# A reordered convolution tail and feed-forward entry in a two-layer decoder step

## What is computed

```python
# layer 0: convolution mixer
a = h @ w_pw1 + b_pw1
u = a[..., :D] * sigmoid(a[..., D:])
y = causal_depthwise_conv(concat(prev, u), w_dw, width=31) + b_dw
y = silu(layernorm(y, ln_g, ln_b))
x = x + m2 * (y @ w_pw2)
# both layers: feed-forward
a = h @ w_up                              # 1024 -> 2 x 2816
x = x + m5 * ((silu(a[..., :F]) * a[..., F:]) @ w_down)
# between the layers: keys and values, blocks of 32 tokens compressed
pr = einsum('bnlkd,lde->bnke', xp, w1[seg]) + einsum('ld,lde->e', pe[seg], w1[seg])
# layer 1: sparse attention on compressed, selected and window keys
```

## Time and profile before

| | us |
|---|---|
| median of 3 runs | 1714.19 |
| lowest, highest | 1709.68, 1717.39 |
| the profiled execution | 1709.89 |
| its span, first to last instruction | 1708.2 |

### The profile page before, as it was taken

How to read it: one execution, slowest core, us unless ns; L and a number is a source line. 1 busy time by engine, 2 the same in 40 slices (tenths; PEclk the granted TensorE clock), 3 DMA queues, 4 the chain that set the end, 5 groups by cost and what they waited for, 6 DMA issues and landing times.

```text
span 1708.2 us, 34694 instructions
## 1 busy us (share of the span) xinstructions
PE 1573.8 (92%) x13817; PEld 1427.1 (84%) x13817; DVE 1144.3 (67%) x2319; ACT 781.7 (46%) x1644; POOL 164.7 (10%) x284
## 2 busy tenths in 40 slices
PE   5888898989999999999999999888898999999996
PEld 3887777989999999989999655455788999999995
DVE  5899976675766858774253467566368676775865
ACT  4545557443453525443224555454344444452544
POOL 2000001000020000002100345333100000000000
PEclk8999999999999999998999999888999999999997
DMA  9889970313645443523322500100232232333321
GB/s 323 273 296 323 303 223 21 88 50 112 198 132 137 124 124 112 146 77 101 79 70 72 153 26 2 50 26 26 75 88 61 63 105 82 100 87 92 95 75 56
DMA packets 236923, 198.40 MB, mean 116 GB/s; under 512 B 7570, under 2 KB 196322, under 8 KB 236496
## 3 DMA queue, kind: packets, MB, share of 16 engines
q1 hardware_dynamic: 225360, 162.81, 31.9%
q0 software_dynamic: 6352, 23.88, 4.7%
q10 hardware_dynamic: 5056, 9.54, 1.7%
HBM read 188.87 MB, written 11.20 MB: 117 GB/s over the span
## 4 chain that ended last, share of the span: by engine, by line
PE 75%; DMA 8%; DVE 7%; ACT 5%; issue 4%; POOL 1%; POOLq 0%; SPq 0%; DVEq 0%; ACTq 0%
PE ps L2215 31%; PE ps L2529 23%; DMA ada<-in_w_ada_dram 6%; PE ps L2195 5%; PE ps L2266 4%; PE ps L2231 3%; PE ps L2663 2%; PE ps L2710 2%; PE ps L2588 2%; DMA xrows<-in_x_sample_dram 1%; DVE t L1483 1%; PE ps L2780 1%; DMA C<-in_cache_kv_dram 1%; PE ps L2564 1%; DVE PT L2115 1%
## 5 line engine op out<-in xcount | busy, mean ns | idle before, releaser
L820 ACT ACTIVATE wh<-raw 128x1024 fp32r<-128x1024 f32 (+2 forms) x129 | 118.6, 921 | 287.7 <-PE ps L2215 263.3
L2529 PE MATMUL ps<-Hh,bh 128*128 128x288 f32 x608 | 179.6, 295 | 2.0 <-DVE t L1887 2.0
L2529 PE MATMUL ps<-Hh,bl 128*128 128x288 f32 x608 | 179.0, 294 | 0.0
L2529 PE MATMUL ps<-Hl,bh 128*128 128x288 f32 x608 | 179.0, 294 | 0.0
L2215 PE MATMUL ps<-Hh,wh 128*128 128x288 f32 (+1 forms) x688 | 156.1, 309 | 13.6 <-DVE wl L1415 9.0
L2215 PE MATMUL ps<-Hl,wh 128*128 128x288 f32 (+1 forms) x688 | 150.7, 301 | 0.0
L2215 PE MATMUL ps<-Hh,wl 128*128 128x288 f32 (+1 forms) x688 | 150.3, 301 | 0.0
L1415 DVE TENSOR_TENSOR wl<-raw,wh 128x1024 fp32r<-128x1024 f32 (+2 forms) x129 | 135.1, 1049 | 14.7 <-ACT wh L820 14.3
L2215 PE MATMUL ps<-ah,wh 128*128 128x288 f32 x656 | 140.8, 296 | 2.2 <-issue 2.1
L2215 PE MATMUL ps<-al,wh 128*128 128x288 f32 x656 | 140.2, 295 | 0.0
L2215 PE MATMUL ps<-ah,wl 128*128 128x288 f32 x656 | 140.2, 295 | 0.0
(11 more groups left out here) (381 smaller groups left out, 3889.7 us busy)
## 6 DMA issues: line engine op xcount, KB each, us to landing
ada<-in_w_ada_dram SPq DMA_DIRECT2D x55, 1024.0 KB, 8.4
raw<-in_ffn_w_up_dram SPq DMA_DIRECT2D x88, 512.0 KB, 4.9
raw<-in_conv_w_pw_dram SPq DMA_DIRECT2D x24, 512.0 KB, 9.2
raw<-in_ffn_w_down_dram SPq DMA_DIRECT2D x32, 384.0 KB, 3.8
raw<-in_ffn_w_down_dram SPq DMA_DIRECT2D x32, 320.0 KB, 3.3
ada<-in_w_ada_dram ACTq DMA_DIRECT2D x9, 1024.0 KB, 7.1
raw<-in_w_kv_dram SPq DMA_DIRECT2D x12, 512.0 KB, 3.9
C<-in_cache_kv_dram POOLq DMA_DIRECT2D x32, 128.0 KB, 3.6
```

The lines of the kernel that those rows point to most:

```text
L820: A(wh[:, u % RING, 0:K, 0:w], raw[:, u % RING, 0:K, 0:w], ACT.Copy).then_inc(hi_ready, 1)
L2529: last = M(ps[:, bank, 0:HT], wt[:, blk, k], rt, start=(j in (0, 1, 2, 6) and k == 0 and i == 0), stop=(k == 3 and i == 2), skip_group_che ...
```

## The change

- Tail of the convolution: y of chunks 0 to 6 is summed by POOL into `mu` (`add_chunk`), PE sums that total and chunk 7 only. Groups 2 and 3 of `up4` and `us4` for chunk 7 are copied by 16 POOL DMAs, groups 0 and 1 by ACT; DVE copies no `us4` for it and writes `stage` instead of ACT. The last strip is turned after the sums and evacuated after the norm. The square root table is loaded before the convolution ends.
- Norms that precede a feed-forward load the silu table once the first half is done.
- Feed-forward entry: on DVE the first split and `product(0)` come after two of the five inner sums, the second split after the third, the third split after the fifth. On ACT the third split comes one place earlier.
- The first pair of a section waits for its banks one by one, by the unit number modulo 3.
- `cmp_bias` is gone; `pe_cmp` becomes 15 more columns of the first hidden product, and ACT takes the bias from one of them.
- `expd` and `tabs` share the semaphore `sel_in`; `slopes` is merged into `const`.

The diff, cut to its core:

```diff
@@ -543,7 +544,7 @@
...
                    8: [("hidden", 1)]}
-        CMP_END = {2: [("bias", 0)], 3: [("turn", 1)], 4: [("turn", 3)], 5: [("keys", 0)], 6: [("turn", 5)],
+        CMP_END = {3: [("turn", 1)], 4: [("turn", 3)], 5: [("keys", 0)], 6: [("turn", 5)],
@@ -690,8 +691,33 @@
...
+            def add_chunk(j):
+                pool.wait_ge(S("conv"), (CW + 1) * (j + 1))
+                pool.wait_ge(S("cs_ev"), j + 1)
+                if j > 1:
+                    pool.wait_ge(S("taps_in"), 2 + j - 1)
+                nc.gpsimd.tensor_tensor(mu[:], y[:, 0, :] if j == 1 else mu[:], y[:, j, :], ALU.add).then_inc(S("taps_in"), 1)
+
+            pool.wait_ge(ada_ev, 4 * (STRIPS_FIRST + 2))
+            for j in range(1, DC - 2):
+                add_chunk(j)
+            pool.wait_ge(S("taps_in"), 2 + DC - 3)
...
             nc.gpsimd.memset(up4[96:P, :, TP + 4 * STEPS - 8:], 0.0).then_inc(S("const"), 1)
+            pool.wait_ge(S("const"), 5)
+            pool.wait_ge(tile_free, U_PW2)
+            for g in range(2, 4):
+                for sh in range(4):
+                    n = min(TP + 4 * STEPS - 4, CW - 1 + TP - sh)
+                    pool.dma_start(up4[32 * sh:32 * sh + 32, g, 0:n], u_p[32 * g:32 * g + 32, DC - 1, sh:sh + n]).then_inc(S("up4_dma"), 16)
+            pool.wait_ge(S("cs_pe"), DC - 1)
+            for g in range(2, 4):
+                for sh in range(4):
+                    n = (CW - 1 + NT - sh) * NB
+                    pool.dma_start(us4[32 * sh:32 * sh + 32, g, 0:n],
+                                   u_s[32 * g:32 * g + 32, DC - 1, sh:, :].rearrange("p t b -> p (t b)")).then_inc(S("us4_dma"), 16)
+            pool.wait_ge(S("const"), 5)
+            add_chunk(DC - 2)
@@ -772,12 +798,12 @@
...
             pool.wait_ge(tile_done, U_WO)
-            pool.dma_start(expd[:], c["expd"]).then_inc(S("expd_in"), 16)
+            pool.dma_start(expd[:], c["expd"]).then_inc(S("sel_in"), 16)
...
-            pool.dma_start(tabs[:], c["tabs"]).then_inc(S("tabs_in"), 16)
+            pool.dma_start(tabs[:], c["tabs"]).then_inc(S("sel_in"), 16)
@@ -943,6 +969,9 @@
...
                 else:
+                    if keeps:
+                        act.wait_ge(S("st_tb"), g + 2 + (g + 1) // 2)
+                        A(scrap[:], epst[:], ACT.Silu).then_inc(S("st_tb"), 1)
@@ -1087,23 +1116,24 @@
...
             act.wait_ge(tile_free, U_PW2)
-            for g in range(4):
+            for g in range(2):
...
                     A(up4[32 * sh:32 * sh + 32, g, 0:n], u_p[32 * g:32 * g + 32, DC - 1, sh:sh + n], ACT.Copy).then_inc(S("up4_in"), 1)
-                if g == 1:
-                    sample_out(DC - 2)
+            sample_out(DC - 2)
+            for g in range(2):
+                for sh in range(4):
+                    n = (CW - 1 + NT - sh) * NB
+                    A(us4[32 * sh:32 * sh + 32, g, 0:n], u_s[32 * g:32 * g + 32, DC - 1, sh:, :].rearrange("p t b -> p (t b)"),
+                      ACT.Copy).then_inc(S("us4_in"), 1)
...
             s_ += STRIPS_TAIL
-            strip_out(None, s_ - 1)
+            A(scrap[:], epst[:], ACT.Sqrt)
...
             sample_out(DC - 1)
-            act.wait_ge(S("cr_pe"), 1)
-            A(stage[0:CW - 1, 0, :].rearrange("p (b f) -> p b f", b=2), ps[0:CW - 1, 0:2, :], ACT.Copy).then_inc(S("cr_ev"), 1)
-            A(stage[0:TS, 1, :].rearrange("p (b f) -> p b f", b=2), ps[0:TS, 2:4, :], ACT.Copy).then_inc(S("cr_ev"), 1)
@@ -1123,8 +1153,7 @@
...
-            A(scrap[:], epst[:], ACT.Sqrt)
-            act.wait_ge(S("ln_pe"), DC)
+            act.wait_ge(S("ln_pe"), 2)
@@ -1134,6 +1163,7 @@
...
             ln_hi(1)
+            strip_out(None, s_ - 1)
@@ -1208,8 +1238,8 @@
...
                 inner_hi(layer, 0)
+                split_hi(u0 + 2 + SPLIT_AHEAD)
                 high(0)
-                split_hi(u0 + 2 + SPLIT_AHEAD)
@@ -1260,23 +1290,19 @@
...
                         act.wait_ge(S("kc_pe"), 1)
+                    if g2 == 0:
+                        A(peb[:, t:t + 1], ps[:, 6 + t, n:n + 1], ACT.Copy).then_inc(S("hc"), 1)
+                        act.wait_ge(S("hc"), 2 * t + 1)
...
-            def cmp_bias():
-                act.wait_ge(S("hp_pe"), 1)
-                A(peb[:], ps[:, 6, 0:2], ACT.Copy).then_inc(S("hc"), 1)
-                act.wait_ge(S("hc"), 1)
-
             def cmp_prompt(t):
-                act.wait_ge(S("hp_pe"), 2 + t)
+                act.wait_ge(S("hp_pe"), 1 + t)
...
                 for what, arg in steps:
-                    if what == "bias":
-                        cmp_bias()
-                    elif what == "turn":
+                    if what == "turn":
@@ -1727,13 +1753,10 @@
...
-            dve.wait_ge(S("cs_pe"), DC - 1)
-            dve.wait_ge(tile_free, U_PW2)
-            for g in range(4):
-                for sh in range(4):
-                    n = (CW - 1 + NT - sh) * NB
-                    V.tensor_copy(us4[32 * sh:32 * sh + 32, g, 0:n],
-                                  u_s[32 * g:32 * g + 32, DC - 1, sh:, :].rearrange("p t b -> p (t b)")).then_inc(S("us4_in"), 1)
+            dve.wait_ge(S("cs_pe"), DC)
+            dve.wait_ge(S("cr_pe"), 1)
+            V.tensor_copy(stage[0:CW - 1, 0, :].rearrange("p (b f) -> p b f", b=2), ps[0:CW - 1, 0:2, :]).then_inc(S("cr_ev"), 1)
+            V.tensor_copy(stage[0:TS, 1, :].rearrange("p (b f) -> p b f", b=2), ps[0:TS, 2:4, :]).then_inc(S("cr_ev"), 1)
@@ -1892,15 +1915,15 @@
...
                 inner_sum(layer, 1)
+                split_lo(u0 + SPLIT_AHEAD)
+                product(0)
                 inner_sum(layer, 2)
+                split_lo(u0 + 1 + SPLIT_AHEAD)
...
                 inner_sum(layer, 4)
-                product(0)
-                split_lo(u0 + SPLIT_AHEAD)
-                split_lo(u0 + 1 + SPLIT_AHEAD)
+                split_lo(u0 + 2 + SPLIT_AHEAD)
...
                 low(0)
-                split_lo(u0 + 2 + SPLIT_AHEAD)
@@ -1991,6 +2014,13 @@
...
+            def offsets():
+                for t, cp in enumerate((CPk, CPv)):
+                    pe_t = vT[:, R_PE + 16 * t:R_PE + 16 * t + 16].rearrange("p (r f) -> p f r", r=2)
+                    V.tensor_copy(cp[:, :, 4 * NKV, 0:2], pe_t)
+                    V.memset(cp[:, :, 4 * NKV, 2:], 0.0)
+
+            offsets()
@@ -2382,7 +2412,9 @@
...
                 pe.wait_ge(S("taps_in") if j < 2 else S("taps_dve"), j + 1 if j < 2 else j - 1)
-                pe.wait_ge(S("us4_in"), 16 * (j + 1))
+                pe.wait_ge(S("us4_in"), 16 * (j + 1) if j < DC - 1 else 16 * j + 8)
+                if j == DC - 1:
+                    pe.wait_ge(S("us4_dma"), 16 * 8)
@@ -2413,19 +2445,11 @@
...
-            def sum_y(cc):
-                pe.wait_ge(S("cs_ev"), cc + 1)
-                pe.wait_ge(S("conv"), (CW + 1) * (cc + 1))
-                sum_chunk(y[:, cc, :], cc, S("ln_pe"), bank=4)
-
-            for cc in range(DC - 2):
-                sum_y(cc)
-
             pe.wait_ge(S("taps_dve"), DC - 2)
-            pe.wait_ge(S("up4_in"), 16)
+            pe.wait_ge(S("up4_in"), 8)
+            pe.wait_ge(S("up4_dma"), 16 * 8)
             pe.wait_ge(S("cs_ev"), DC - 1)
-            turn_strip(s_ - 1)
-            pe.wait_ge(ada_ev, 4 * s_)
+            pe.wait_ge(ada_ev, 4 * (s_ - 1))
@@ -2433,10 +2457,12 @@
...
             convs += 1
-            sum_y(DC - 2)
+            pe.wait_ge(S("taps_in"), 2 + DC - 2)
+            sum_chunk(mu, 0, S("ln_pe"), n=2, bank=4)
...
             pe.wait_ge(S("pc_ev"), 1)
-            sum_chunk(y[:, DC - 1, :], DC - 1, S("ln_pe"), bank=4)
+            sum_chunk(y[:, DC - 1, :], 1, S("ln_pe"), n=2, bank=4)
+            turn_strip(s_ - 1)
@@ -2499,8 +2525,11 @@
...
                         if j == 0:
-                            pe.wait_ge(tile_free, q.before)
+                            pe.wait_ge(tile_free, q.before - (q.before % RING > 0))
                         elif j == 2:
+                            pe.wait_ge(tile_free, q.before + (q.before % RING == 1))
+                    elif q.i == 1:
+                        if j == 0:
@@ -2556,24 +2585,16 @@
...
-            def cmp_bias():
-                pe.wait_ge(S("w1_in"), 32)
-                pe.wait_ge(S("st_rms"), 5)
-                for t in range(2):
-                    for j in range(LC // 2):
-                        last = M(ps[:, 6, t:t + 1], w1s[t][:, j, :], vT[:, R_PE + 16 * t + j:R_PE + 16 * t + j + 1],
-                                 start=(j == 0), stop=(j == LC // 2 - 1))
-                last.then_inc(S("hp_pe"), 1)
-                pe.wait_ge(S("hc"), 1)
-
...
                 pe.wait_ge(S(f"cc_in{b % 2}"), 64 * (b // 2 + 1))
+                if b == 0:
+                    pe.wait_ge(S("st_rms"), 5)
...
                     pe.wait_ge(S("kc_dve"), 2)
-                    pe.wait_ge(S("hc"), 3)
+                    pe.wait_ge(S("hc"), 4)
@@ -2582,23 +2603,25 @@
...
                 pe.wait_ge(S("cp_act"), 4 * g2 + 4)
-                n = 4 * NKV * NCS
```

(13 more changed lines are left out.)

33 lines of the change are left out of this document (16 added, 17 removed).

## The result

The changed kernel takes 1696.42 us, median of four runs (1694.59 to 1700.01), against 1715.79 of the kernel before, ratio 0.9898, 95% interval 0.9868 to 0.9929. A second group gave 1696.49 against 1716.08, ratio 0.9882 (0.9849 to 0.9916). So the change makes the kernel faster by 1.0 to 1.2%, 19.4 to 19.6 us by the medians, where the forecast had 23.8. The forecast of 1688.0 was 8.4 too low; the measured time lies in its range of 1680 to 1698 and outside of its own forecast's 1683 to 1693.

What follows compares the result with a forecast made beforehand. It took PE's own work, three quarters of the span, and PE's standstills as the bound; terms for tail, feed-forward entries, key/value projection and attention start summed to -23.8 us, giving 1688, range 1680 to 1698 (8 in 10).

Steps and rivals of the forecast that it cites:

- start of the prompt convolution: Convolution tail: with fewer ACT copies and the sums off PE, the last prompt convolution starts at 244.7, not 248.79: -4.1.
- square root table: End of the convolution tail: table load and dummy activation move into ACT's idle time before the convolution ends: -1.5.
- entry of feed-forward 0, PE's start: Feed-forward 0 entry: with the new DVE order and early silu table, PE starts at 356.74, not 360.78: -4.0.
- clock and bank wait behind it: Feed-forward 0 after its entry: full clock with a 0.6 gap, -2.2, and the first pair's bank wait gone, -0.8.
- keys and values: Key and value projection: bias products go, hidden product grows 0.8, full clock returns; nothing is late next: -11.3.
- attention: wait, clock: Attention start: the gate product waits for tabs too, +4.5, and the idle drops the clock, +1.4.
- entry of feed-forward 1: Second feed-forward entry: PE starts 4.0 earlier and full clock gives 1.8; no bank gain.
- hidden by ACT: Convolution tail: the eight up4 transfers end at 242 to 243 (doubled bound 244.1), before ACT is done; no cost.
- The rival of late transfers: Convolution tail: up4 transfers end at 249, leaving only the table gain: -19.7, about 1692; 13%.
- The two on tabs: Attention start: wait for tabs absorbed, -29.7, about 1682, 10%; or costs +12 instead of 5.9, about 1694, 12%.
- The one on the order at the entries: Feed-forward entries: half of each 4.0 and the clock return as a wait one unit later; about 1694; 8%.
- The one that ends slower: Convolution tail: POOL's 16 SBUF copies run one after another, +60; kernel about 1751, slower than before; 3%.

Runs made afterwards that it cites:

- b_order: Kernel before with only the new order of splits, product and sums on VectorE and ScalarE at both feed-forward entries; 1710.98 us, ratio 0.9955.
- b_bias: Kernel before with only the bias folded into the first hidden product; 1700.52 us, ratio 0.9897.
- c_pages: Changed kernel with the gate product waiting for expd alone and the turns of the cache pages spread; 1680.75 us, ratio 0.9777.
- a_expd: Changed kernel with tabs on another semaphore, so the gate product waits for expd alone; 1692.39 us.
- a_oldentry: Changed kernel with the old order of splits, product and sums at both feed-forward entries, silu table still early; 1707.82 us, ratio 0.9954 to the kernel before.
- a_thin: Changed kernel with five of POOL's six adds cut to one column; 1693.66 us, ratio 0.988 to the kernel before.
- c_filler: c_pages plus ten unused products of y with ones on PE before the last prompt convolution; 1678.27 us, ratio 0.9798 to the kernel before.
- f_short: c_pages plus five unused products on PE before the last prompt convolution; 1679.59 us, ratio 0.9815 to the kernel before.

## Why the prediction was right and wrong

Each term of the sum against what the stages show. "Measured" is the mean with the edit less the mean without it, over the profiles above that differ in nothing else in that stage.

| term | forecast | measured |
|---|---|---|
| start of the prompt convolution | -4.1 | -3.8 |
| square root table | -1.5 | -0.2 |
| clock in the sums of squares | 0 | -1.7 |
| entry of feed-forward 0, PE's start | -4.0 | -3.8 |
| clock and bank wait behind it | -3.0 | -2.4 |
| given back up to keys and values | 0 | +1.4 |
| keys and values | -11.3 | -8.4 |
| attention: wait, clock | +4.5, +1.4 | +4.9, +1.7 |
| entry of feed-forward 1 | -5.8 | -5.3 |
| from there to the end | 0 | +0.4 |
| sum | -23.8 | -17.2 |

The timings say 19.4 and 19.6, with intervals that reach from 12 to 26.

**The base, 4.0 of the 8.4.** "The profiled run took 1709.9 ... the median of the three runs is 4.3 higher ... I take the middle". The middle, 1711.8 as it stands in the forecast (1688 + 23.8), was too low: the median of before was 1715.8 with one run more, and 1712 to 1722 in four groups. The profiled execution was 0.2 above the lowest of the three shown, and a profile at the lower end is no evidence on the level of the next runs. The median less 23.8 would have been 1690.4.

**The rest, 4.4, is the effect.** The step that failed is "What is late next is nothing", for keys and values, and with it the term of 11.3, which measured 8.4 (9.3 if b_order, which has no edit in this stage, is counted with the kernels before). The weights were there, but I did not ask for the pages of the cache, though PE's waits for them stand in the trace of before, at the fourth and the eighth turn:

```profile
806.53 1.09 PE L2195 MATMUL ps<-ident,C 128*128 128x128 f32 x8 [1.38 <-DMA C<-in_cache_kv_dram]
844.54 1.09 PE L2195 MATMUL ps<-ident,C 128*128 128x128 f32 x8 [1.54 <-DMA C<-in_cache_kv_dram]
```

The removal and the fold are right: the first turn comes 12.1 earlier (39.47 becomes 27.35; 9.86 + 0.26 + 2.0 were summed), the stretch that holds the hidden product takes 0.8 more (20.01 becomes 20.83), and b_bias gives 11.9 alone. In the changed kernel the two page waits are 2.0 to 3.1 each and behind one or both of them the clock falls (the eight turns took 1.97 instead of 1.09 at 825.45): the stage is 3.5 longer than in b_bias. c_pages takes the waits away and finds 6.4. That the removal makes them longer is not shown, and two profiles speak against it: b_bias has the removal and short waits, b_order has none and long ones. First b_bias, then b_order:

```profile
801.19 1.09 PE L2199 MATMUL ps<-ident,C 128*128 128x128 f32 x8 [1.54 <-DMA C<-in_cache_kv_dram]
803.36 1.36 PE L2195 MATMUL ps<-ident,C 128*128 128x128 f32 x8 [2.47 <-DMA C<-in_cache_kv_dram]
```

Against b_order the changed kernel's stage is 11.2 shorter, against before b_bias's is 11.9 shorter. So the removal is worth what was forecast either way; what is missing is a wait that the sum held constant and that came out longer. Why is open, below.

**The clock term was put in the wrong places.** I gave the clock back where a long wait goes, and this held at both entries (46.98 against 48.88 with nothing else changed) and behind tabs. I did not ask the same question where work is removed: the six sums that leave PE had kept it busy up to the last prompt convolution. With an idle of 2.5 to 3.2 before it, that convolution took 8.61 to 8.77 (four profiles), with 0.6 to 1.5 it took 7.07 in seven of eight. The eighth is a_expd, 9.35 behind an idle of 0.98:

```profile
245.29 0.44 PE L2225 MATMUL ps<-ident,adarow 128*128 128x128 f32 x1 [2.21 <-issue]
```

There the granted clock was 0.50 from 244.5 on, behind this wait, and had not come back when the convolution began at 250.12; a_oldentry, with 2.13 in the same place and 1.45 before its convolution, was at 1.00 again by then and took 7.07. So the idle right before is not all that counts, and a trace's own PEclk has to be read. In five of the seven profiles of kernels with the change's tail and no added work, the table's 1.5 was gone. In the other direction, the wait before the sums of squares fell from 3.07 to 1.55 and those sums went from 9.69 to 8.00, which was not in the forecast either:

```profile
261.97 9.69 PE L2444 MATMUL ps<-sqb,ones 128*128 128x288 f32 x32 [3.07 <-ACT sqb L1112]
```

(this is the kernel before). The two cancel, and the stage's sum of 5.7 is right against 5.6 by luck.

**The transfers of up4** were said to be "hidden by ACT", ending at 242 to 243. They landed 6.4 to 6.7 after their issues, the last issued at 240.2, so at 246.96, 10.8 after the gating that they wait for; ScalarE was done at 247.02. My doubled bound, 10.4 after the gating, was nearly right, and the value that I took, 8 to 9, was not: the cover was 0.1 and not 2. In c_pages, where they took up to 7.9, the last landed at 249.26 and the convolution began at 249.46, 1.4 after ScalarE was done. The rows name ACT as the releaser, but in all seven profiles with these eight transfers and an idle PE the convolution began 0.20 to 0.21 after the last landing, and 0.15 to 1.37 after ScalarE was done. Before, it began 0.05 to 0.06 after ScalarE. "The forecast is wrong if the convolution starts on a transfer": it does, and the term came out at 3.8 only because the landing and ScalarE nearly meet.

**The adds on POOL.** The hold was right: 4.4 in all against "up to 4.3", and the last gating still had 3.12 of idle before it. What I took for POOL's own time, 1.0 per pass, was 1.4 to 18.8. No cost of it shows: nobody waits for five of them, and a_thin, where the loop is not held, starts its sample convolution no earlier than the scatter. The Trainium skill (SBUF — State Buffer, SBUF: two separate sides) says that the port pair shared by the two engines is locked by whichever starts first, for its whole instruction, and the other blocks fully. The trace agrees where POOL got through: a VectorE add was stretched from 0.69 to 1.79. It shows more than the page where POOL did not: a one-column add lasted 8.86, over some fifteen instructions of VectorE's loop, and not over one.

**The entries and the gates** were right in mechanism and size. At the entries PE starts 0.39 after its last work instead of 4.50; of the two parts of the clock and bank term, 1.9 is clock (b_order) and 0.5 the bank wait, forecast 2.2 and 0.8. The postponed sums cost nothing. From the entry to keys and values only 1.0 of the 2.4 was left: PE waited 2.18 for a strip of modulation weights at 445.01, where it had waited 0.35 before. This wait was 0.2 to 0.7 in the four profiles without the change's tail; with it, 1.7 to 2.3 in eight and 0.3 and 0.7 in c_filler and f_short. It is 2.21 in a_oldentry, so the order at the entry does not make it; what does I did not test apart. The gate product's wait for tabs was 6.07, within the "4 to 6" to a tenth, and was neither absorbed nor doubled. tabs landed in 6.6; by the Trainium skill's fit (DMA: Bandwidth & Descriptors, Anatomy of one DMA), the estimate of 5.0, the cost would have been 3.2, and the measured 4.9 decides.

**The rivals.** None was the case in full. The rival of late transfers had the right place, but not the price (10.35 to 11.57 to the convolution, where it wanted 14.5). The two on tabs fell: the wait was neither absorbed nor worth 12, but 6.7. The one on the order at the entries fell: no wait came back within the three units. The one that ends slower fell: the eight copies of up4 landed 6.4 to 6.7 after their own issue, 0.5 apart, not one after another.

**What stays open.** Page waits of 1.4 to 1.6 in before (twice) and b_bias, 2.0 to 3.1 in b_order, a_oldentry and the five with the whole entry change and the old turns. The stage sum, 17.2, and the timings, 19.4 and 19.6, differ by 2, which their intervals cover. The issues of POOL for the first waiting page stand at the same distance from the turns, within 0.3; the longest landing was 5.3 (before) and 5.5 (b_bias) against 6.0 (the changed kernel) and 6.1 (b_order). The weight transfer that SyncE issues 6.7 after the first turn is under way beside them in each: it took 4.9 (before), 5.1 (b_bias), 5.3 (the changed kernel) and 6.3 (b_order), so the transfers are slower together; what slows them no run tells. b_bias and b_order have one profile each. Neither the fold nor the entry order alone decides it. c_pages makes the question idle for this kernel.

## What to carry to other kernels

Make the sum against the median of many runs and use the profile for differences only; a second profile of the same kernel tells which stretches scatter (here 7 us in two of them) and may not be read. Where a wait or work leaves PE, ask both questions of every stretch behind it: which transfer becomes the next late one, with the distance from its release, and whether PE now stands idle where it was busy (here 2.5 us and more), since work that is taken off PE can be what kept its clock. Two loads may share a semaphore only if every waiter needs the later one.
